# Hybrid mixer of a fused two-block kernel: weight slabs between the attention steps, the output projection in two parts, low parts of weights on VectorE

## The reference, cut to what matters

```python
def even_mixer(h, w_in, w_out, dw_w, dw_b, ln_g, ln_b):
    """Stick-breaking attention heads || Conformer conv channels. h: (B,S,D)."""
    proj = h @ w_in
    q, k, v, u, gate = jnp.split(
        proj, [SB_WIDTH, 2 * SB_WIDTH, 3 * SB_WIDTH, 3 * SB_WIDTH + CONV_CH], axis=-1)
    a_out = merge_heads(stick_breaking_attention(
        split_heads(q, SB_HEADS), split_heads(k, SB_HEADS), split_heads(v, SB_HEADS)))
    c = u * jax.nn.sigmoid(gate)
    c = causal_depthwise_conv(c, dw_w, dw_b)
    c = jax.nn.silu(layer_norm(c, ln_g, ln_b))
    return jnp.concatenate([a_out.astype(h.dtype), c], axis=-1) @ w_out
```

## Time and profile before

| | us |
|---|---|
| median of 3 runs | 1763.93 |
| the profiled execution, its own time | 1765.37 |
| its span in the profile | 1763.3 |
| TensorE busy with matmuls | 1676.9 (95%) |
| VectorE busy | 1065.5 (60%) |
| ScalarE busy | 847.4 (48%) |
| GpSimd busy | 176.2 (10%) |

### The profile page before, as it was taken

One profiled execution on the slowest core, in us unless ns is written; L12 is line 12 of the kernel. 1 busy time (PEld: TensorE's weight loads), 2 busy tenths in 40 slices (PEclk: granted clock), 3 DMA queues, 4 the chain that ended last, 5 costly groups with the idle time before them and its releaser, 6 DMA issues. The chain is left out here.

```text
span 1763.3 us, 28914 instructions
## 1 busy us (share of the span) xinstructions
PE 1676.9 (95%) x11809; PEld 1562.4 (89%) x11818; DVE 1065.5 (60%) x1484; ACT 847.4 (48%) x1137; POOL 176.2 (10%) x48
## 2 busy tenths in 40 slices
PE   7999999999999998999988589999999999899998
PEld 6998999989799997999987479999899989889997
DVE  1796776747567766544539955545644475765444
ACT  6323655543665546444454364444544465354443
POOL 5351000021600000000057200000000000000000
PEclk9999999989999999999999699999999999999999
DMA  8623477643236563655642315556355644425552
GB/s 268 201 72 97 159 196 215 192 142 122 92 121 204 169 218 122 197 189 174 214 150 96 96 36 193 189 190 215 132 191 188 204 151 163 143 86 190 189 180 83
DMA packets 220068, 283.49 MB, mean 161 GB/s; under 512 B 13004, under 2 KB 197315, under 8 KB 219987
## 3 DMA queue, kind: packets, MB, share of 16 engines
q1 hardware_dynamic: 218499, 278.18, 48.7%
q10 hardware_dynamic: 1488, 4.17, 0.7%
HBM read 280.88 MB, written 1.44 MB: 160 GB/s over the span
## 5 line engine op out<-in xcount | busy, mean ns | idle before, releaser
L1561 PE MATMUL ps<-x_hi,w_hi 128*128 128x256 f32 (+1 forms) x2368 | 672.8, 284 | 1.1 <-POOL w_lo L469 0.8
L1562 PE MATMUL ps<-x_lo,w_hi 128*128 128x256 f32 (+1 forms) x2368 | 671.6, 284 | 0.0
L1563 PE MATMUL ps<-x_hi,w_lo 128*128 128x256 f32 (+1 forms) x2368 | 671.5, 284 | 0.0
L547 ACT ACTIVATE w_hi<-raw 128x2048 fp32r<-128x2048 f32 x262 | 498.8, 1911 | 219.3 <-PE ps L1563 199.8
L1108 DVE TENSOR_TENSOR w_lo<-raw,w_hi 128x2048 fp32r<-128x2048 f32 x162 | 371.3, 2292 | 260.3 <-ACT w_hi L547 260.3
L1561 PEld LDWEIGHTS ps<-x_hi,w_hi 128*128 128x128 f32 (+1 forms) x2368 | 455.4, 192 | 5.9 <-issue 2.7
L1562 PEld LDWEIGHTS ps<-x_lo,w_hi 128*128 128x128 f32 (+1 forms) x2368 | 455.3, 192 | 2.3
L1563 PEld LDWEIGHTS ps<-x_hi,w_lo 128*128 128x128 f32 (+1 forms) x2368 | 455.1, 192 | 0.2
L1561 PE MATMUL ps<-w_hi,x_hi 128*128 128x256 f32 (+3 forms) x688 | 222.0, 323 | 16.3 <-DVE x_lo L1001 13.4
L469 POOL TENSOR_TENSOR w_lo<-raw,w_hi 128x2048 fp32r<-128x2048 f32 x32 | 160.1, 5026 | 759.0 <-ACT w_hi L547 759.0
L1562 PE MATMUL ps<-w_lo,x_hi 128*128 128x256 f32 (+3 forms) x688 | 216.7, 315 | 0.0
(11 more groups left out here) (172 smaller groups left out, 1373.3 us busy)
## 6 DMA issues: line engine op xcount, KB each, us to landing
raw<-in_ffn_w_in SPq DMA_DIRECT2D x88, 1024.0 KB, 5.1
raw<-in_ffn_w_up SPq DMA_DIRECT2D x44, 1024.0 KB, 5.1
raw<-in_ffn_w_out SPq DMA_DIRECT2D x44, 1024.0 KB, 4.9
raw<-in_ffn_w_down SPq DMA_DIRECT2D x22, 1024.0 KB, 5.0
raw<-in_hgrn_w_in SPq DMA_DIRECT2D x16, 1024.0 KB, 5.9
raw<-in_gla_w_in SPq DMA_DIRECT2D x12, 1024.0 KB, 5.5
raw<-in_hyb_w_in SPq DMA_DIRECT2D x10, 1024.0 KB, 5.2
raw<-in_dsa_w_in SPq DMA_DIRECT2D x6, 1024.0 KB, 5.4
```

The lines of the kernel that those rows point to most:

```text
L547: act.activation(w_hi[slot][:, :], raw[slot][:, :], ACT.Copy).then_inc(hi_done[slot], 1)
L1561: pe.matmul(out_ap, a_hi, b_hi, start=start, stop=False, skip_group_check=True)
L1562: pe.matmul(out_ap, a_hi, b_lo, start=False, stop=False, skip_group_check=True)
L1563: return pe.matmul(out_ap, a_lo, b_hi, start=False, stop=stop, skip_group_check=True)
```

## The change

The ten input slabs come in the order `HYB_IN`: v0, v1, u0, gate0, q0, k0, u1, gate1, q1, k1 (slots 0, 1, 2, 3, 2, 3, 0, 1, 2, 3). TensorE multiplies both v slabs for token block 0 before block 1 is transposed, and puts u1, gate1, q1 and k1 between the attention steps of the first pairs. The two last pairs go through together. `project_out` gets a range of chunks: chunks 0 to 3 of both blocks now stand ahead of `conv_turned`, chunks 4 to 7 behind the transposes, and the transposes of the next FFN's block 0 stand after the last chunk instead of between the chunks of block 1. VectorE makes eleven low parts of this stage (one of them, `early`, inside the end of the FFN before) and GpSimd one. The convolution goes by halves of two channel chunks, so that the second half needs u1 and gate1 only later. ScalarE's sigmoids, copies, exponentials and high parts are put in the same order, two table loads are made earlier (`preload`).

```diff
+HYB_IN = ((0, 4), (1, 5), (2, 6), (3, 8), (2, 0), (3, 2), (0, 7), (1, 9), (2, 1), (3, 3))
...
-            load_four_columns(hyb_in, 6 * SLAB, 1)
-            load_four_columns(hyb_in, 0, 1)
-            for s in range(2):
-                load(s, [(raw_cols(s), col_slab(hyb_in, 4 * SLAB + s * SLAB))])
+            for s, col0 in HYB_IN:
+                load(s, [(raw_cols(s), col_slab(hyb_in, col0 * SLAB))])
...
-            ring.skip(0, 1)
-            ring.skip(1, 1)
-            for s in (2, 3, 0, 1, 2, 3, 0, 1, 2, 3, 0, 1):
-                low_one(s)
+            for s, n in ((0, 3), (1, 3), (2, 1), (3, 4)):
+                ring.skip(s, n)
+            low_one(2)
+            ring.skip(2, 2)
...
                     add_normed_block(1)
+                    if early is not None:
+                        low_one(early)
                 scaled_block(1)
...
-                    convolve(TAPS_AHEAD)
-                    for pair in range(SB_HEADS // 2):
-                        for hd in (2 * pair, 2 * pair + 1):
-                            stick_bound(hd)
-                        convolve(TAPS_BETWEEN)
-                        for hd in (2 * pair, 2 * pair + 1):
-                            stick_softplus(hd)
-                        convolve(TAPS_BETWEEN)
-                    assert not taps
...
+                    low_one(3)
+                    gated_half(0, 2, 3)
+                    convolve(3)
+                    low_one(3)
+                    convolve(2)
+                    low_one(0)
+                    low_one(1)
+                    convolve(9)
+                    low_one(2)
+                    convolve(7)
+                    bounds(0)
+                    low_one(3)
+                    convolve(6)
+                    softplus(0)
+                    convolve(5)
+                    bounds(1)
+                    convolve(12)
+                    softplus(1)
...
+                    convolve(CONV_TAPS * 2 - (3 + 2 + 9 + 7 + 6 + 5 + 12))
+                    gated_half(1, 0, 1)
+                    low_one(0)
+                    low_one(1)
+                    convolve(16)
+                    low_one(2)
+                    bounds(2)
+                    bounds(3)
+                    convolve(11)
+                    softplus(2)
+                    softplus(3)
+                    convolve(16)
+                    low_of_banks(2)
+                    low_one(3)
+                    convolve(CONV_CHUNKS * CONV_TAPS)
...
+                    half_token_slab(0, 0, x0, 0)
+                    half_token_slab(1, 0, None, 1)
+                    turn_block(1)
+                    slab_into(4, 2, x1)
+                    slab_into(5, 3)
+                    half_token_slab(0, 1, None, 0)
+                    half_token_slab(1, 1, None, 1)
+                    slab_into(6, 2)
+                    slab_into(7, 3)
+                    all_copied()
...
+                    heads(stick_logits, 0)
+                    slab_into(4, 0)
+                    heads(stick_logits, 1)
+                    slab_into(5, 1)
+                    heads(stick_rest, 0)
+                    slab_into(6, 2)
+                    for s in range(2):
+                        pe.wait_ge(proj_free[s], made[s] + 1)
+                    heads(stick_values, 0)
+                    heads(stick_rest, 1)
+                    slab_into(7, 3)
+                    all_copied()
+                    heads(stick_logits, 2)
+                    heads(stick_logits, 3)
+                    heads(stick_values, 1)
+                    keep_warm(2 * WARM_STEP)
+                    heads(stick_rest, 2)
+                    heads(stick_rest, 3)
+                    keep_warm(WARM_STEP)
+                    heads(stick_values, 2)
+                    heads(stick_values, 3)
+
+                    base = x_new(6)
+                    project_out(HYB_OUT, lambda tb, k: base + k // 2 + 1, ks=range(4))
+                    conv_turned()
+                    keep_warm(WARM_NORMED, 4)
...
-                    base = x_new(6)
-                    project_out(HYB_OUT, lambda tb, k: base + (k // 2 + 1 if k < 4 else k - 1),
-                                {(1, 5): lambda: turn_after(0, base + 6)})
+                    project_out(HYB_OUT, lambda tb, k: base + k - 1, ks=range(4, NK))
+                    turn_after(0, base + 6)
```

More of the change, by code:

```diff
@@ new lines, in stick_weights @@
+                    def stick_weights(pair):
+                        for hd in (2 * pair, 2 * pair + 1):
+                            act.wait_ge(sb_rest, hd + 1)
+                            if hd >= 4:
+                                act.wait_ge(sb_pv, hd - 3)
+                            act.activation(hyb["w"][:, hd % 4, :], ps[:, hd % 4, 0:3 * P], ACT.Exp).then_inc(sb_w, 1)
+                    made[2] += 1
+                    high_one(2)
+                    sigmoid_gate(3, 0)
+                    high_one(3)
@@ L1077, in residual_ffn, with after_ffn @@
                 split_normed(1, *norm)
[L1079 removed]
+            def after_ffn(f, norm, normed=False, early=None):
                 last = FFN_SLOTS[f][1]
@@ L1667, in project_out @@
                             ins.then_inc(slab_used[s], 1)
-                for s in slots:
+                for s in slots[ks.start // 2:ks.stop // 2]:
                     used[s] += 1
```

165 lines of the change are left out of this document (80 added, 85 removed).

## The result

The changed kernel takes 1750.24 us (median of 4 runs, 1747.78 to 1750.39), beside 1763.74 us for the kernel before on the same chip (4 runs, 1763.34 to 1767.48). The ratio is 0.9905, interval 0.9888 to 0.9922: faster by 13.5 us. Measured once more, on another chip, it was 1746.35 us (5 runs, 1745.36 to 1748.95) beside 1767.18 (11 runs), ratio 0.9888 (0.9868 to 0.9908): faster by 20.8 us. Both intervals leave out 1, and both gains are under 2%. The forecast was 1742.5 in 1737 to 1751. Both medians lie in the range, and both are above the point.

A forecast was written before the change was run, and what follows sets the result against it. In the attention part VectorE works while TensorE waits, with 28.5 us lost on taps beside GpSimd's low parts. Step by step, block 0's square moves from 1032.0 to 1010.4, 21.6 us off the median 1763.93: 1742.5, range 1737 to 1751.

The forecast's parts named there:

- The cause: VectorE's convolution taps: one meeting a GpSimd low part waits for it whole, through a shared port lock; 28.5 us lost.
- Rival 3: VectorE's stretched taps come from transfers or other memory sharing, so 28.5 us stay: 1771 us, slower; chance 0.03.
- Rival 2: VectorE's taps become slower, 476 ns instead of 405 on 103 taps, 7.3 us more: 1750 us; chance 0.06.
- Rival 4: Mixer's weight slabs: one comes late, so the reorder doesn't take effect: 1761 us, no change to speak of; chance 0.03.
- The sum up to the rests: VectorE's work up to the softplus of the last two pairs, put at 975.7; TensorE's rests follow.
- VectorE's sum: VectorE continuously busy from first bounds to last tap: taps, low parts, bounds and waits together 64.4 us, ending at 994.7.
- The way from the rests to the first product of the output: Four rests, weights, values, a high part and copies after the softplus at 975.7; chunk 0 ready at about 983.
- The lower clock: TensorE in the output projection after gaps: 1.5 us added for the first half, 0.8 us for the second.
- The convolution branch: Transposes, statistics, root, normalisation and back transposes to the first `x_lo` of chunk 4: 8.5 us, TensorE going on at 1004.0.
- Rival 1: The clock stays low in the last third: 8 us above the forecast, 1750.5 us, up to 1756; chance 0.12.
- half of the output projection ahead of the convolution: Mixer's end: eight chunk steps, 10.9 us at full clock, done by 995.5, leaving TensorE 5.5 us less before the square.
- the v halves: Mixer's start: v products of block 0 fill TensorE's 4.24 us gap; gain 5.76 us, cost 0.4, so 5.3.

The follow-up runs named there:

- e1: Changed kernel, but GpSimd makes the ten low parts that VectorE makes inside the mixer: mixer 143.18 us, whole 1760.95 us, ratio 0.9963.
- e4: Kernel before, old order, GpSimd computing only 16 of 2048 columns of each of its twelve mixer low parts: mixer 141.24 us, whole 1759.78 us, ratio 0.9953.
- after_again: The changed kernel unedited, timed in more rounds on another chip, with a second profiled execution: mixer 130.50 us, whole 1746.35 us, ratio 0.9888.
- e3: Changed kernel with the output projection in one piece again behind the back transposes: mixer 130.76 us, whole 1748.20 us, ratio 0.9895.
- e6: Changed kernel with more matmuls on zeros ahead of last rests, output projection and back transposes, and behind these: mixer 126.74 us, whole 1741.14 us, ratio 0.9870.
- e9: Changed kernel with the output projection in four pieces around the convolution, without eight matmuls on zeros: mixer 128.05 us, whole 1742.31 us, ratio 0.9862.
- e10: Changed kernel with four projection pieces, matmuls on zeros in gaps, and VectorE's last two low parts later: mixer 125.87 us, whole 1742.49 us, ratio 0.9869.
- e11: Changed kernel with VectorE's last two low parts moved behind the last tap and behind the normalisation: mixer 130.60 us, whole 1745.13 us, ratio 0.9884.
- before, again: The kernel before, unedited, profiled in one more execution: mixer 150.99 us, whole 1768.46 us.
- e7: Changed kernel without the v products of block 0 ahead of block 1's transposes; they come after gate0: mixer 137.81 us, whole 1754.66 us, ratio 0.9939.
- e2: Kernel before, old order, with all twelve low parts of the mixer on VectorE: mixer 142.07 us, whole 1758.77 us, ratio 0.9950.

## Why the prediction was right, and by how much it was off

**The cause** held. Taps are long beside GpSimd's low parts and at no other time: 0.40 us each after, 1.54 in e1 (29.35 / 19), and none of 120 above 484 ns in e4, where only the low parts are short. Nor are transfers the cause: in the changed kernel nine taps from 923.10 take 3.65 us while transfers move 407 GB/s:

```profile
923.10:926.75 3.65, 3.65 (x32) 3.65 (x32) 3.65 (x11) 2.40 (x2) 0.00 (x0) 1.00 1.02 407
```

Rival 3 falls, and with it the only way to a slower kernel. Rival 2 falls with the taps' 0.40 us. Rival 4 does not occur: no slab had TensorE waiting. The prediction read one half of the blocking only. Its sentence that a tap which meets a low part waits for it whole doesn't hold for the 28 taps from 950.21 to 961.37. It counted the low parts from 950.11 as four equal ones; the first took 15.65 us because the taps held it off (e4's section). The 28.5 us lost on VectorE are right all the same.

**The schedule** held step by step (3.57 us taken off the times after). One of the agreements is luck, as told below the table:

| step | forecast | measured |
|---|---|---|
| v products begin | 889.4 | 889.5 |
| first softplus of the last two pairs done, rests begin | 975.7 | 975.7 |
| last tap ends | 994.7 | 994.3 |
| chunk 0 ready, output projection begins | 983 | 984.1 |
| its first half ends | 995.5 | 996.7 |
| TensorE goes on behind the convolution | 1004.0 | 1005.1 |
| square of block 0 | 1010.4 | 1012.2 |
| square to next FFN's block 1 | 22.5 | 22.5 |

*The luck.* In after_again the rests begin at 974.1 on this scale, and so they do in e3, e6, e9, e10 and e11. The sum up to the rests was 1.6 us too long, and the clock drop at the first pair's logits, which it had not foreseen, made up for 1.55 of it in the one profiled execution of the result. VectorE's sum is also not all that decides there: e11 takes 2.2 us of VectorE's work from ahead of the last bounds, and the rests begin no earlier, because TensorE's logits are ready no earlier.

*The mis-sized terms* are at the end. The way from the rests to the first product of the output took 8.4 us at a granted clock of 1.00, where I gave it 7.3: 1.1 more. The lower clock cost 12.6 less 10.9 = 1.7 us in the first half, where I had 1.5, and 1008.67 to 1015.80 less 5.6 = 1.5 us in the second, where I had 0.8. The convolution branch took 8.4 for 8.5. Together 1.8 us: 19.8 instead of 21.6. e6 confirms the clock's share by taking it away.

**Rival 1 is not what happened**, though the first measurement (1750.24) is the very time that it named. The clock's excess over the forecast is 0.9 us in the two halves and 1.5 us at the first pair's logits, not 8. The other part of the miss in that measurement lies in stages that the change doesn't touch. Between the same kind of events, the profiled executions show (us):

| stage | before | before, again | after | after_again |
|---|---|---|---|---|
| the first block's `dsa_mixer` | 113.61 | 115.55 | 115.53 | 112.39 |
| FFN ahead of the mixer | 182.47 | 182.47 | 183.99 | 182.46 |
| a later FFN of the same kind | 182.47 | 183.96 | 183.96 | 182.47 |
| the mixer of the change | 151.05 | 150.99 | 131.25 | 130.50 |

In the profiled pair of the first measurement these three cost the changed kernel 1.9, 1.5 and 1.5 us. In before, again, two of the three are at the long value as well. Over all fourteen profiled executions, of both kernels and all experiments, the first stage took about 112.4 us in six, 113.6 in three and 115.5 in five, and the later FFN 182.5 in eight and 184.0 in six, whichever order the mixer had. Only the FFN ahead of the mixer had its long value in one execution alone, the first of the changed kernel; after_again had the short one. So nothing ties the long values to the new code. The second measurement, whose profiled execution met the short ones of these three, gave 20.8.

**The step of the argument that was wrong** without cost for the sum: that half of the output projection ahead of the convolution brings the end forward. e3 takes it out and its mixer is as long (130.76, beside 131.25 and 130.50). Of the 19.8 us, the v halves bring 6.6, or 7.3 against after_again (e7); the forecast had 5.3. The rest comes from the low parts' new engine together with the slabs between the attention steps, which the runs don't divide further: alone they bring 9.0 (e2, taken as a lower bound) and 7.9 (e1, with the v halves in it).

Three versions have mixers 2.5 to 5.4 us shorter than the changed kernel's: e6_more_warm, e9_pieces and e10_combined. As whole kernels all three beat the kernel before, and their intervals overlap the changed kernel's 0.9868 to 0.9908, so that they beat the changed kernel as well isn't shown. Only e10_combined stood beside it on one chip: five of its six runs are below all five of the latter's (from 1745.36), the sixth is above them.

## What to carry to other kernels

When a short instruction on VectorE has a maximum that equals the length of some GpSimd instruction, look for the overlap before counting either engine's work, and look at the longest GpSimd instruction too, for it can be the one kept out. Here moving 25 us of work from the idle engine to the busy one made the busy one's total smaller. Put a dense block of products into a wait only if nothing on the critical path is queued behind it, and choose the pieces that the next consumer needs first. Judge a change by the stage between two events that both kernels share; the whole span here carried 5 us from stages with the same instructions.

## What was unexpected

A 128 x 16 subtraction on GpSimd, 0.22 us by itself, took 18.57 us beside an unbroken run of taps (e4). The kernel before already had such a case, a low part of 15.65 us beside taps of the usual length.

Stages with the same instructions come in a few fixed lengths: 112.4, 113.6 and 115.5 for one, 182.5 and 184.0 for another. A further one, from the square at 1531.8 to that at 1552.0 before (20.2 us), took 22.9 us in after_again. The second can be followed in one pair of executions. The same stretch of FFN products, just ahead of the mixer, in windows of the kernel before and of the kernel after:

```profile
692.00:703.00 11.00, 9.27 (x64) 9.00 (x64) 6.74 (x17) 8.11 (x18) 0.00 (x0) 0.84 0.00 0
703.00:706.00 3.00, 1.92 (x16) 1.75 (x15) 2.15 (x9) 3.00 (x11) 0.00 (x0) 1.00 0.53 161
706.00:710.00 4.00, 4.00 (x36) 4.00 (x35) 4.00 (x3) 1.66 (x1) 0.00 (x0) 1.00 0.16 34
```

```profile
694.00:705.00 11.00, 8.13 (x64) 7.53 (x64) 6.74 (x17) 8.10 (x18) 0.00 (x0) 1.00 0.02 3
705.00:708.00 3.00, 1.70 (x13) 1.70 (x14) 2.10 (x9) 3.00 (x11) 0.00 (x0) 0.97 0.52 171
708.00:712.00 4.00, 4.00 (x24) 4.00 (x23) 4.00 (x3) 1.70 (x1) 0.00 (x0) 0.60 0.12 14
```

Before, the 64 matmuls of the first window ran partly at the lower level (0.84) and the dense part behind them at the full one. After, the first ran at full clock, finished sooner, and TensorE waited longer for the next block (2.40 us instead of 1.08). Then the dense part ran at 0.60 for 4 us, with 24 matmuls where before had 36. Here being early was of no use, and the clock fell in the part that counts. Which of the two an execution meets was not under the control of any run here.
